# Stick-breaking attention of a two-block fp32 kernel: TensorE's order alternates from step to step, and the weighing moves two steps behind the transposes

## The chip, the cores and the metric

The kernel runs on one core of one Trainium2 chip. The metric is the device time of one execution in microseconds (us). One execution runs two transformer-like blocks over 2048 tokens of width 1024, all in float32; the change touches one stage of the first block, the stick-breaking attention.

## The reference, cut to the stage that changes

```python
SEQ, N_HEADS, HEAD_DIM, Q_BLOCK = 2048, 8, 64, 128

def _stick_breaking_attention(q, k, v):
    ...
    for blk in range(n_blocks):
        q0 = blk * Q_BLOCK
        kl = q0 + Q_BLOCK
        qb = qf[:, :, q0:kl]
        z = jnp.einsum("bhqd,bhkd->bhqk", qb, kf[:, :, :kl]) * scale
        q_pos = q0 + jnp.arange(Q_BLOCK)
        mask = jnp.arange(kl)[None, :] < q_pos[:, None]
        log_one_minus = jnp.where(mask, jax.nn.log_sigmoid(-z), 0.0)
        rev = lax.cumsum(log_one_minus, axis=3, reverse=True)
        weights = jnp.exp(jnp.where(mask, z + rev, -jnp.inf))
        outs.append(jnp.einsum("bhqk,bhkd->bhqd", weights, vf[:, :, :kl]))
    ...

def first_block(...):
    ...  # a gated short convolution, then k, v, q and g by projections
    o = _stick_breaking_attention(q, k, v)
    x = x + (o * jax.nn.silu(g)) @ w_out_b[j]
    return _rmsnorm(x, norm_f)
```

The kernel uses that the running product of sigmoid(-z) from the right, P, gives the weights as differences P(k+1) - P(k). It multiplies P with differences of neighbouring values instead, so the weights themselves are never formed.

## The kernel before

The kernel runs its stages one after another: the mixer (Strassen products), its output product, projections, then **the stick-breaking stage** (`phase_stick`), the stage's output product, the second block's projection, its selection and attention, and the last output product.

In the stick-breaking stage the 8 heads are taken as 4 *head pairs*. For each head pair the 16 blocks of 128 queries follow each other, and the keys of a block are cut into chunks of at most 512, the one with the diagonal first. One (head pair, query block, chunk) is a **unit**: 40 per head pair, 160 in all. Counted from a head pair's start, units 0, 1, 2, 3 are blocks of one unit each with 128, 256, 384 and 512 keys; blocks of two units follow (unit 4 has 128 keys and unit 5 has 512; 6 and 7 have 256 and 512; and so on), then blocks of three from unit 12 and of four from unit 24. A block's first unit *opens* it and its last one *closes* it; only the first of a block can be shorter than 512. The last unit of the head pair before is called unit -1 here.

Each unit passes five engines' hands, for its two heads (`s` = 0, 1):

1. **scores** on TensorE (L1650): three products of split fp32 parts for each of two heads, into one of four PSUM buffers `z`;
2. **soften** on ScalarE (L1525): sigmoid from `z` into `soft`; for the unit that opens a block GpSimd then masks the diagonal (L1504);
3. **multiply** on VectorE (L1598): a scan over the unit for each head, `soft` into `prod`, with the carry of the unit before it in the block;
4. **transposes** on TensorE (L1668) of `prod` into `turn`, and **leave** on ScalarE (L1534) from there into `prob`;
5. **weighing** on TensorE (L1689): `prob` with the values' differences into the block's output `o_ps`. There are two such PSUM buffers, one for even and one for odd blocks. When a block is closed, VectorE copies it out with an addition (`leave` in its section, L1608, "the copy-out" below). The weighing of a unit that opens block b waits for the copy-out of block b-2 (`o_left`).

Every engine's section is a loop over steps `t`, written out in order; an engine executes its list in that order and waits on semaphores. Before, step t of TensorE is: scores(t+2), transposes(t), at some steps transposes of values, weighing(t-1). ScalarE's step is soften(t+2), leave(t); VectorE's is multiply(t+1), and copy-out(t-2) where unit t-2 closes a block. So scores run two steps ahead of the transposes.

Four times per head pair, at steps 4 and 12 of it and 8 and 5 steps before its start, a quarter of the keys, queries and values is prepared (`chores_at`): ScalarE makes `k_hi`, `q_hi` at the end of the step (L1516, L1518), VectorE makes `k_lo`, `q_lo`, `v_step` (L1574, L1576, L1580), and a step later TensorE transposes the values (`transpose_v`, L1676, "values' transposes" below) through the same two `turn` buffers. `turn_free` makes each use of a `turn` buffer wait until ScalarE has emptied the one two uses before.

Of the kernel before, what the change touches and what calls it, by code (L numbers as in the profile page):

```python
# [1360 lines left out]
def phase_stick(nc, sem, kvqg_t, o_t, ident, loaded, space, w_out_b, x1, mod_row, norm_w, head_norms):  # L1361
# [11 lines left out]
    U = len(units)  # L1373
# [8 lines left out]
    def closes(u):  # L1382
        return units[u][2] == 0
# [27 lines left out]
    with ExitStack() as ctx:  # L1411
# [95 lines left out]
        @block.scalar  # L1507
        def _(act):
            nc.scalar.preload_act_table(ACT.Sigmoid)

            def split(n, pair, piece):
                j, cols = pair % 2, piece_cols(piece)
                if pair >= 2:
                    act.wait_ge(z_ready, 2 * EACH * (pair - 1))
                act.wait_ge(k_in[piece], 16 * (pair + 1))
                nc.scalar.activation(k_hi[:, j, cols], k_raw[:, cols], ACT.Copy).then_inc(kh_done, 1)  # L1516
                act.wait_ge(q_in[piece], 16 * (pair + 1))
                nc.scalar.activation(q_hi[:, j, cols], q_raw[:, cols], ACT.Copy).then_inc(qh_done, 1)  # L1518

            def soften(u, s):  # L1520
                n = units[u][3]
                act.wait_ge(z_ready, 2 * u + s + 1)
                if u >= DEEP:
                    act.wait_ge(multiplied, 2 * (u - DEEP) + s + 1)
                nc.scalar.activation(soft[:, u % DEEP, s, 0:n], z[u % 2 * 2 + s][:, 0:n], ACT.Sigmoid, scale=-SCALE).then_inc(softened, 1)  # L1525

            def leave(u, s):
                n = units[u][3]
                act.wait_ge(turned, 2 * u + s + 1)
                if u == 0:  # L1530
                    act.wait_ge(loaded.upper_out, 16 * TILES)
                if u >= DEEP:
                    act.wait_ge(weighed, u - DEEP + 1)
                nc.scalar.activation(prob[:, u % DEEP, s, 0:n], turn[turn_of["unit", u, s] % 2][:, 0:n], ACT.Copy).then_inc(p_ready, 1)  # L1534

            def leave_v(n, pair, piece):
                act.wait_ge(v_turned, n + 1)
                if pair >= 2:
                    act.wait_ge(weighed, EACH * (pair - 1))
                nc.scalar.activation(v_nat[:, pair % 2, piece * 4:piece * 4 + 4].rearrange("p a b -> p (a b)"),  # L1540
                                     turn[turn_of["v", n] % 2][:], ACT.Copy).then_inc(v_left, 1)

            def split_weights(k):
                act.wait_ge(space.w_in[k], 16)
                nc.scalar.activation(space.w_hi[:, k], space.w_raw[:, k], ACT.Copy).then_inc(space.w_hi_done, 1)

            for t in range(-2, U + 2):
                if t in weights_at:
                    split_weights(weights_at.index(t))
                if t in outputs_at:  # L1550
                    space.high(nc, act, outputs_at.index(t))
                if t == -2:
                    for c in chores_at(t):
                        split(*c)
                if 0 <= t + 2 < U:
                    for s in range(2):
                        soften(t + 2, s)
                if 0 <= t < U:
                    for s in range(2):
                        leave(t, s)  # L1560
                for c in chores_at(t - 1):
                    leave_v(*c)
                if t > -2:
                    for c in chores_at(t):
                        split(*c)

        @block.vector
        def _(dve):
# [31 lines left out]
            def leave(u):  # L1600
                pair, qb, _, _ = units[u]
                j, last = pair % 2, P * (qb + 1)
                dve.wait_ge(weighed, u + 1)
                if u == 0:
                    dve.wait_ge(loaded.lower_out, 16 * TILES)
                if pair >= 2:
                    dve.wait_ge(o_out[qb * P // PIECE], 16 * (pair - 1))
                nc.vector.tensor_scalar(o_sb[:, j, qb * P:last], o_ps[block_of[u] % 2][:, 0:P], v_raw[:, j, last:last + 1], None,  # L1608
                                        ALU.add).then_inc(o_left, 1)
# [2 lines left out]
                dve.wait_ge(space.w_hi_done, k + 1)  # L1612
                nc.vector.tensor_tensor(space.w_lo[:, k], space.w_raw[:, k], space.w_hi[:, k].bitcast(F32), ALU.subtract).then_inc(space.w_lo_done, 1)

            for t in range(-2, U + 2):
                if t == weights_at[0]:
                    dve.wait_ge(space.cols_in, 48)
                    nc.vector.scalar_tensor_tensor(space.cols[:, 0], space.cols[:, 0], 1.0, space.cols[:, 1], ALU.add, ALU.mult).then_inc(space.scale_made, 1)
                if t - 1 in weights_at:
                    split_weights(weights_at.index(t - 1))  # L1620
                if t + 1 in outputs_at:
                    space.gate(nc, dve, outputs_at.index(t + 1))
                if t - 1 in outputs_at:
                    space.low(nc, dve, outputs_at.index(t - 1))
                if t == -2:
                    for c in chores_at(t):
                        split(*c)
                if 0 <= t + 1 < U:
                    for s in range(2):
                        multiply(t + 1, s)  # L1630
                if 0 <= t - 2 < U and closes(t - 2):
                    leave(t - 2)
                if t > -2:
                    for c in chores_at(t):
                        split(*c)

        @block.tensor
        def _(pe):
# [40 lines left out]
            def weigh(u):  # L1679
                pair, qb, at, n = units[u]  # L1680
                o = o_ps[block_of[u] % 2]
                pe.wait_ge(p_ready, 2 * u + 2)
                pe.wait_ge(v_left, pair * PIECES + qb * P // PIECE + 1)
                if opens(u) and block_of[u] >= 2:
                    pe.wait_ge(o_left, block_of[u] - 1)
                for c in range(0, n, P):
                    for s in range(2):
                        rows_s = slice(s * HD, s * HD + HD)
                        ins = nc.tensor.matmul(o[rows_s, 0:P], v_nat[:, pair % 2, (at + c) // P, rows_s], prob[:, u % DEEP, s, c:c + P],  # L1689
                                               start=opens(u) and c == 0, stop=closes(u) and c + P == n)  # L1690
                ins.then_inc(weighed, 1)

            for t in range(-2, U + 2):
                if 0 <= t + 2 < U:
                    scores(t + 2)
                if 0 <= t < U:
                    for s in range(2):
                        transpose(t, s)
                for c in chores_at(t - 1):
                    transpose_v(*c)  # L1700
                if 0 <= t - 1 < U:
                    weigh(t - 1)


def phase_out_b(nc, sem, space, x1, o_t, kvqg_t, norm_f, ident, xf, xt_hi, xt_lo, xt_raw, next_w, next_ps):
# [1742 lines left out]
```

## Time and profile before

| what | us |
|---|---|
| median of 3 runs | 3191.09 |
| lowest and highest run | 3189.61, 3191.92 |
| span of the profiled execution | 3189.0 |
| TensorE busy in the span (matmuls) | 2990.2 |
| VectorE busy | 2253.7 |
| ScalarE busy | 1624.1 |
| stick-breaking stage, first scores to the last weighing | 1198.1 to 1641.5 |

The profiled execution's own span is 2.1 us under the median of the runs. The stage takes 443.4 us of it, 14%. TensorE's rows come as matmuls (PE) and weight loads (PEld). A matmul's end is modelled, so for the pace of TensorE the starts are read, and best those of the weight loads: each matmul has one, and the distance from the first load of one group to the first load of the next is the time that the group takes. In the profile the weighing shows two hardware matmuls for each one of the program.

### The profile page before, as it was taken

The numbers are of one execution on the slowest core, as the hardware profiler recorded it, in microseconds if no ns is written. First come the engines' busy times: TensorE is split into PE (matmuls) and PEld (weight loads), VectorE is DVE, ScalarE is ACT, GpSimd is POOL, SyncE is SP. The second block draws the span as 40 slices with busy tenths as digits, with TensorE's granted clock in tenths as the row PEclk, the third lists the DMA queues.
The fourth block names the chain that finished last, engine by engine and source line by source line (L and its number), as shares of the span: only waits on it lengthen the run. The fifth ranks groups of instructions, "written<-read, shape, count | busy, mean of one in ns | idle before, by whom it ended". The sixth has DMA issues, their size and how long they took to land. (4 is left out here: it accounts for less than half of the span.)

```text
span 3189.0 us, 48176 instructions
## 1 busy us (share of the span) xinstructions
PE 2990.2 (94%) x17460; PEld 2369.3 (74%) x17460; DVE 2253.7 (71%) x3296; ACT 1624.1 (51%) x2947; POOL 231.3 (7%) x519
## 2 busy tenths in 40 slices
PE   6999999999998999999999999999977889998899
PEld 5888788888777866677777777887756666776687
DVE  8888877753677758888878554524378989988543
ACT  5344422232545436777769423211288887887500
POOL 0000000000000001110100000000021321213100
PEclk8999999999999999999999999999989999999899
DMA  4434422244657432111136334232641111011665
GB/s 119 121 109 122 145 67 75 84 141 144 170 171 254 154 131 77 32 37 41 45 92 199 112 96 132 86 132 74 172 98 34 31 28 24 23 36 39 170 183 158
DMA packets 377860, 331.47 MB, mean 104 GB/s; under 512 B 100988, under 2 KB 331900, under 8 KB 371472
## 3 DMA queue, kind: packets, MB, share of 16 engines
q1 hardware_dynamic: 371784, 293.40, 32.4%
q0 software_dynamic: 5120, 34.67, 2.8%
q8 instruction: 142, 2.33, 0.3%
q14 instruction: 94, 0.77, 0.1%
q10 hardware_dynamic: 720, 0.31, 0.1%
HBM read 211.26 MB, written 107.10 MB: 100 GB/s over the span
## 5 line engine op out<-in xcount | busy, mean ns | idle before, releaser
L629 PE MATMUL p_oa_acc<-s_h_a_hi,s_mx_w_hi 128*128 128x512 f32 x768 | 301.8, 393 | 15.2 <-DVE s_h_a_lo L418 9.4
L323 ACT ACTIVATE s_mx_w_hi<-s_mx_raw 128x512 fp32r<-128x512 f32 x224 | 139.1, 629 | 320.6 <-PE p_oa_acc L629 256.8
L629 PE MATMUL p_oa_acc<-s_h_a_lo,s_mx_w_hi 128*128 128x512 f32 x768 | 300.4, 391 | 0.0
L629 PE MATMUL p_oa_acc<-s_h_a_hi,s_mx_w_lo 128*128 128x512 f32 x768 | 300.2, 391 | 0.0
L1598 DVE TENSOR_TENSOR_SCAN s_st_prod<-s_st_soft,s_st_prod 128x512 f32<-128x512 f32 x192 | 234.4, 1267 | 15.9 <-ACT s_st_soft L1525 15.9
L3174 PE MATMUL p_sa_turn<-s_ident,s_sa_arg 128*128 128x128 f32 x1088 | 166.3, 289 | 48.5 <-ACT s_sa_prob L2783 30.9
L1525 ACT ACTIVATE s_st_soft<-p_st_z 128x512 f32<-128x512 f32 (+3 forms) x320 | 153.7, 534 | 112.0 <-PE p_st_z L1650 112.0
L2345 PE MATMUL p_pr_ps<-s_h_hi,s_pr_w_hi 128*128 128x512 f32 (+1 forms) x712 | 195.4, 395 | 1.8 <-PEq L1712 1.2
L2766 ACT ACTIVATE s_sa_arg<-s_sa_arg,s_sa_low_top 128x128 f32<-128x128 f32 (+15 forms) x128 | 155.7, 1218 | 79.6 <-DVE s_sa_low_top L2918 79.6
L460 DVE TENSOR_TENSOR s_mx_w_lo<-s_mx_raw,s_mx_w_hi 128x512 fp32r<-128x512 f32 x224 | 153.5, 685 | 57.8 <-ACT s_mx_w_hi L323 56.3
L2345 PE MATMUL p_pr_ps<-s_h_lo,s_pr_w_hi 128*128 128x512 f32 (+1 forms) x712 | 191.5, 389 | 0.0
L2345 PE MATMUL p_pr_ps<-s_h_hi,s_pr_w_lo 128*128 128x512 f32 (+1 forms) x712 | 191.5, 389 | 0.0
L3174 PEld LDWEIGHTS p_sa_turn<-s_ident,s_sa_arg 128*128 128x128 f32 x1088 | 120.9, 145 | 86.4 <-issue 53.3
L2227 DVE TENSOR_TENSOR s_pr_w_lo<-s_pr_raw,s_pr_w_hi 128x1024 fp32r<-128x1024 f32 (+1 forms) x22 | 26.5, 1204 | 223.5 <-ACT s_pr_w_hi L2168 223.5
L629 PEld LDWEIGHTS p_oa_acc<-s_h_a_hi,s_mx_w_hi 128*128 128x128 f32 x768 | 145.0, 189 | 47.9 <-issue 17.9
L2775 ACT ACTIVATE s_sa_relu<-p_sa_pr 128x512 f32<-128x512 f32 (+3 forms) x304 | 155.5, 567 | 28.0 <-DVE s_sa_score L2899 13.8
L629 PEld LDWEIGHTS p_oa_acc<-s_h_a_hi,s_mx_w_lo 128*128 128x128 f32 x768 | 145.1, 189 | 30.4
L3188 PE MATMUL p_sa_o_sum<-s_sa_prob,s_sa_v_nat 128*64 128x128 f32 x2176 | 160.7, 288 | 7.4 <-ACT s_sa_o L2789 7.4
L629 PEld LDWEIGHTS p_oa_acc<-s_h_a_lo,s_mx_w_hi 128*128 128x128 f32 x768 | 145.2, 189 | 29.6
L2899 DVE SCALAR_TENSOR_TENSOR s_sa_score<-s_sa_relu,s_sa_w_idx,s_sa_score 128x1024 f32<-128x1024 f32 (+7 forms) x154 | 153.8, 1021 | 18.9 <-ACT s_sa_relu L2775 17.9
L3188 PEld LDWEIGHTS p_sa_o_sum<-s_sa_prob,s_sa_v_nat 128*64 128x64 f32 x2176 | 121.2, 141 | 58.9 <-issue 46.3
L2783 ACT ACTIVATE s_sa_prob<-p_sa_turn 128x512 f32<-128x512 f32 (+3 forms) x320 | 154.3, 541 | 11.2 <-PE p_sa_turn L3174 10.7
(379 smaller groups left out, 7408.7 us busy)
## 6 DMA issues: line engine op xcount, KB each, us to landing
s_mx_raw<-in_w_in_a SPq DMA_DIRECT2D x128, 256.0 KB, 3.8
s_pb_ada<-in_w_ada SPq DMA_DIRECT2D x16, 768.0 KB, 4.3
s_pr_raw<-in_w_in SPq DMA_DIRECT2D x21, 512.0 KB, 3.9
s_pr_work<-s_pr_stage SPq DMA_DIRECT2D x38, 256.0 KB, 4.2
d_rot_hi<-s_pr_rot POOLq DMA_DIRECT2D x9, 1024.0 KB, 4.3
d_rot_lo<-s_pr_stage POOLq DMA_DIRECT2D x9, 1024.0 KB, 6.2
d_y_t<-s_mx_y SPq DMA_DIRECT2D x16, 512.0 KB, 5.5
s_oa_y_raw<-d_y_t SPq DMA_DIRECT2D x16, 512.0 KB, 4.8
```

The source lines that it names most:

```text
L323: nc.scalar.activation(w_hi[:, m], raw[g % 2][:, m], ACT.Copy).then_inc(hi_done, 1)
L460: nc.vector.tensor_tensor(w_lo[:, m], raw[g % 2][:, m], w_hi[:, m].bitcast(F32), ALU.subtract).then_inc(lo_done, 1)
L629: ins = nc.tensor.matmul(bank, w[:, m, k, :], a[:, m, k, :], start=(k == 0 and n == 0), stop=(k == KH - 1 and n == 2))
L1525: nc.scalar.activation(soft[:, u % DEEP, s, 0:n], z[u % 2 * 2 + s][:, 0:n], ACT.Sigmoid, scale=-SCALE).then_inc(softened, 1)
L1598: nc.vector.tensor_tensor_scan(prod[:, b, s, 0:n][:, ::-1], back, back, carry, ALU.mult, ALU.bypass).then_inc(multiplied, 1)
L2345: ins = nc.tensor.matmul(ps[b % 2][0:cols, t * 512:(t + 1) * 512], w[b % 2][:, k, 0:cols], a[:, k, t * 512:(t + 1) * 512], start=(k == 0 a ...
L2766: nc.scalar.activation(row, row, ACT.Exp, scale=-1.0, bias=low_top[:, s % DEEP, side, len(parts(qb)) - 1:len(parts(qb))], accum_out=total[ ...
L2775: nc.scalar.activation(relu[:, a % R_DEEP, half:half + n], pr[p % BANKS][:, 0:n], ACT.Relu).then_inc(relu_done, 1)
L2783: nc.scalar.activation(prob[:, u % P_DEEP, side, 0:w], turn[turn_of["prob", u, side] % 2][:, 0:w], ACT.Copy).then_inc(p_ready, 1)
L2899: ins = nc.vector.scalar_tensor_tensor(s, relu[:, a % R_DEEP, 0:n], w, s, ALU.mult, ALU.add)
L3174: ins = nc.tensor.transpose(turn[i % 2][:, c:c + P], arg[:, s % DEEP, side, at + c:at + c + P], ident[:])
L3188: ins = nc.tensor.matmul(o_ps[side * HD:side * HD + HD, pair * P:pair * P + P], v_nat[:, (at + c) // P, kv * HD:kv * HD + HD], prob[:, u % ...
```

## The change

TensorE's steps alternate. At even t the order is scores(t+2), transposes(t), weighing(t-2); at odd t it is weighing(t-2), transposes(t), scores(t+2). The weighing is one step later than it was. ScalarE's order follows: at odd t soften(t+2) stands behind leave(t). VectorE's copy-out moves from step t = u+2 to t = u+3 for a unit u, so one more pair of scans stands ahead of it. No instruction is added or removed, and sizes, buffers and semaphore targets stay.

```diff
@@ scalar
-                if 0 <= t + 2 < U:
+                if 0 <= t + 2 < U and t % 2 == 0:
                     for s in range(2):
                         soften(t + 2, s)
                 if 0 <= t < U:
@@
                 for c in chores_at(t - 1):
                     leave_v(*c)
+                if 0 <= t + 2 < U and t % 2:
+                    for s in range(2):
+                        soften(t + 2, s)
@@ vector
-            for t in range(-2, U + 2):
+            for t in range(-2, U + 3):
@@
-                if 0 <= t - 2 < U and closes(t - 2):
-                    leave(t - 2)
+                if 0 <= t - 3 < U and closes(t - 3):
+                    leave(t - 3)
@@ tensor
             for t in range(-2, U + 2):
-                if 0 <= t + 2 < U:
+                if 0 <= t - 2 < U and t % 2:
+                    weigh(t - 2)
+                if 0 <= t + 2 < U and t % 2 == 0:
                     scores(t + 2)
                 if 0 <= t < U:
                     for s in range(2):
                         transpose(t, s)
                 for c in chores_at(t - 1):
                     transpose_v(*c)
-                if 0 <= t - 1 < U:
-                    weigh(t - 1)
+                if 0 <= t + 2 < U and t % 2:
+                    scores(t + 2)
+                if 0 <= t - 2 < U and t % 2 == 0:
+                    weigh(t - 2)
```

The first place is TensorE at the start of a head pair (line numbers of the changed kernel are 3 higher). `p_st_z` are scores, `p_st_turn` transposes, `p_st_o` the weighing; a unit of 128 keys has 2 transposes and 2 weighing products, one of 512 has 8 of each. Before, from the transposes of unit 1 to the weighing of unit 2:

```order
L1668 MATMUL p_st_turn<-s_ident,s_st_prod 128x128 x4
L1689 MATMUL p_st_o<-s_st_prob,s_st_v_nat 64x128 x2
L1650 MATMUL p_st_z<-s_st_k_hi,s_st_q_hi 128x128 x2
L1650 MATMUL p_st_z<-s_st_k_lo,s_st_q_hi 128x128 x2
L1650 MATMUL p_st_z<-s_st_k_hi,s_st_q_lo 128x128 x2
L1668 MATMUL p_st_turn<-s_ident,s_st_prod 128x128 x6
L1689 MATMUL p_st_o<-s_st_prob,s_st_v_nat 64x128 x4
L1650 MATMUL p_st_z<-s_st_k_hi,s_st_q_hi 128x512 x2
L1650 MATMUL p_st_z<-s_st_k_lo,s_st_q_hi 128x512 x2
L1650 MATMUL p_st_z<-s_st_k_hi,s_st_q_lo 128x512 x2
L1668 MATMUL p_st_turn<-s_ident,s_st_prod 128x128 x8
L1689 MATMUL p_st_o<-s_st_prob,s_st_v_nat 64x128 x6
```

The same engine and place after the change, from the transposes of unit 1 to those of unit 3:

```order
L1671 MATMUL p_st_turn<-s_ident,s_st_prod 128x128 x4
L1653 MATMUL p_st_z<-s_st_k_hi,s_st_q_hi 128x512 x2
L1653 MATMUL p_st_z<-s_st_k_lo,s_st_q_hi 128x512 x2
L1653 MATMUL p_st_z<-s_st_k_hi,s_st_q_lo 128x512 x2
L1653 MATMUL p_st_z<-s_st_k_hi,s_st_q_hi 128x128 x2
L1653 MATMUL p_st_z<-s_st_k_lo,s_st_q_hi 128x128 x2
L1653 MATMUL p_st_z<-s_st_k_hi,s_st_q_lo 128x128 x2
L1671 MATMUL p_st_turn<-s_ident,s_st_prod 128x128 x6
L1692 MATMUL p_st_o<-s_st_prob,s_st_v_nat 64x128 x6
L1671 MATMUL p_st_turn<-s_ident,s_st_prod 128x128 x8
```

The scores of units 3 and 4 now stand together, and so do the weighings of units 0 and 1 (2 and 4 products in one row of 6); the weighing of unit 1 stands ahead of the transposes of unit 3.

The second place is VectorE there: `s_st_prod` are the scans (two in a row for one unit, 128, 256, 384, 512, 128 and 512 keys), `s_st_o` the copy-outs of units -1, 0 and 1. Before:

```order
L1598 SCALAR_TENSOR_TENSOR s_st_prod<-s_st_soft 128x256 x2
L1598 SCALAR_TENSOR_TENSOR s_st_prod<-s_st_soft 128x384 x2
L1608 TENSOR_SCALAR s_st_o<-p_st_o,s_st_v_raw 128x128
L1598 SCALAR_TENSOR_TENSOR s_st_prod<-s_st_soft 128x512 x2
L1608 TENSOR_SCALAR s_st_o<-p_st_o,s_st_v_raw 128x128
L1598 SCALAR_TENSOR_TENSOR s_st_prod<-s_st_soft 128x128 x2
L1608 TENSOR_SCALAR s_st_o<-p_st_o,s_st_v_raw 128x128
L1598 SCALAR_TENSOR_TENSOR s_st_prod<-s_st_soft,s_st_prod 128x512 x2
```

After:

```order
L1601 SCALAR_TENSOR_TENSOR s_st_prod<-s_st_soft 128x256 x2
L1601 SCALAR_TENSOR_TENSOR s_st_prod<-s_st_soft 128x384 x2
L1601 SCALAR_TENSOR_TENSOR s_st_prod<-s_st_soft 128x512 x2
L1611 TENSOR_SCALAR s_st_o<-p_st_o,s_st_v_raw 128x128
L1601 SCALAR_TENSOR_TENSOR s_st_prod<-s_st_soft 128x128 x2
L1611 TENSOR_SCALAR s_st_o<-p_st_o,s_st_v_raw 128x128
L1601 SCALAR_TENSOR_TENSOR s_st_prod<-s_st_soft,s_st_prod 128x512 x2
L1611 TENSOR_SCALAR s_st_o<-p_st_o,s_st_v_raw 128x128
```

The copy-out of unit -1 now stands behind the scans of unit 3, and that of unit 1 behind those of unit 5.

## Rows read from the trace of the kernel before

**Rows 1.** The page's first part: busy us (share) xinstructions of each engine.

```profile
PE 2990.2 (94%) x17460; PEld 2369.3 (74%) x17460; DVE 2253.7 (71%) x3296; ACT 1624.1 (51%) x2947; POOL 231.3 (7%) x519
```

**Rows 2.** Busy time by stretch: the stage, then its second and third head pair.

```profile
core 0: us, PE busy (x) PEld busy (x) DVE busy (x) ACT busy (x) POOL busy (x), PEclk, DMA share, GB/s
1198.10:1641.50 443.40, 428.77 (x4288) 315.72 (x4288) 379.47 (x438) 319.26 (x692) 42.31 (x64) 0.99 0.15 42
1311.68:1422.70 111.02, 106.60 (x1074) 78.36 (x1072) 97.98 (x115) 82.48 (x176) 12.88 (x16) 1.00 0.16 40
1422.70:1533.70 111.00, 107.57 (x1084) 79.26 (x1083) 93.91 (x110) 79.80 (x175) 10.43 (x17) 1.00 0.14 39
```

**Rows 3.** Waits in the stage: us in total, times, longest us.

```profile
ACT s_st_soft L1525 <- PE p_st_z L1650: 112.0, 138, 1.9
...
PEld p_st_turn L1676 <- ACT s_st_prob L1534: 16.9, 15, 1.7
...
PE p_st_turn L1676 <- DVE s_st_v_step L1580: 6.6, 5, 1.4
```

**Rows 4.** Timeline, one full step: start us, us, engine, line, operation, xcount.

```profile
1589.54 4.79 DVE L1598 TENSOR_TENSOR_SCAN s_st_prod<-s_st_soft,s_st_prod 128x512 f32<-128x512 f32 x4
...
1590.23 0.19 PEld L1650 LDWEIGHTS p_st_z<-s_st_k_hi,s_st_q_hi 64*128 64x128 f32 x2 [0.17 <-issue]
...
1590.57 0.39 PE L1650 MATMUL p_st_z<-s_st_k_lo,s_st_q_hi 64*128 64x512 f32 x2
1590.57 0.19 PEld L1650 LDWEIGHTS p_st_z<-s_st_k_hi,s_st_q_lo 64*128 64x128 f32 x2
1590.80 0.39 PE L1650 MATMUL p_st_z<-s_st_k_hi,s_st_q_lo 64*128 64x512 f32 x2
1591.13 0.86 PEld L1668 LDWEIGHTS p_st_turn<-s_ident,s_st_prod 128*128 128x128 f32 x8 [0.37 <-issue]
...
1591.23 1.09 ACT L1525 ACTIVATE s_st_soft<-p_st_z 128x512 f32<-128x512 f32 x2 [0.88 <-PE p_st_z L1650]
1592.15 0.85 PEld L1689 LDWEIGHTS p_st_o<-s_st_prob,s_st_v_nat 128*64 128x64 f32 x16 [0.17 <-issue]
...
1593.17 0.19 PEld L1650 LDWEIGHTS p_st_z<-s_st_k_hi,s_st_q_hi 64*128 64x128 f32 x2 [0.17 <-issue]
```

**Rows 5.** Timeline, the stage's end, where no scores are left.

```profile
1636.72 0.86 PEld L1668 LDWEIGHTS p_st_turn<-s_ident,s_st_prod 128*128 128x128 f32 x8 [0.17 <-issue]
...
1637.74 0.85 PEld L1689 LDWEIGHTS p_st_o<-s_st_prob,s_st_v_nat 128*64 128x64 f32 x16 [0.17 <-issue]
...
1639.79 1.73 PEld L1689 LDWEIGHTS p_st_o<-s_st_prob,s_st_v_nat 128*64 128x64 f32 x32 [0.17 <-issue]
```

**Rows 6.** Timeline, scores behind transposes: the stage's start, and the selection stage.

```profile
1199.72 0.72 PEld L1676 LDWEIGHTS p_st_turn<-s_ident,s_st_v_step 128*128 128x128 f32 x4 [0.22 <-issue]
...
1200.77 0.29 PEld L1650 LDWEIGHTS p_st_z<-s_st_k_hi,s_st_q_hi 64*128 64x128 f32 x2 [0.33 <-issue]
...
2700.36 1.09 PE L3174 MATMUL p_sa_turn<-s_ident,s_sa_arg 128*128 128x128 f32 x8
2701.21 0.48 PE L3152 MATMUL p_sa_pr<-s_sa_ki_qi_q 128*128 128x512 f32 x1
```

**Rows 7.** Timeline, the second head pair's start.

```profile
1311.68 1.09 PE L1668 MATMUL p_st_turn<-s_ident,s_st_prod 128*128 128x128 f32 x8
...
1316.84 1.09 ACT L1525 ACTIVATE s_st_soft<-p_st_z 128x512 f32<-128x512 f32 x2 [1.07 <-PE p_st_z L1650]
...
1318.57 2.50 DVE L1598 TENSOR_TENSOR_SCAN s_st_prod<-s_st_soft 128x512 f32<-128x512 f32 x2 [0.45 <-issue]
1320.99 0.32 DVE L1608 TENSOR_SCALAR s_st_o<-p_st_o,s_st_v_raw 128x128 f32<-128x128 f32 x1
...
1325.44 1.09 PE L1668 MATMUL p_st_turn<-s_ident,s_st_prod 128*128 128x128 f32 x8
1327.17 0.66 PE L1676 MATMUL p_st_turn<-s_ident,s_st_v_step 128*128 128x128 f32 x4 [0.64 <-ACT s_st_prob L1534]
```

## The prediction, made before the changed kernel was run

> **What bounds the kernel now.** I read the page's engine part first: TensorE is busy 94% of the span, VectorE 71% [rows 1]. Then the stretches of the stage: in its 443.4 us TensorE's matmuls fill 428.8 and VectorE 379.5 [rows 2]. TensorE is the bound, but VectorE has only 64 us to spare in 160 steps. Then the waits: the only waits of TensorE that matter are for the values' transposes, some 16.9 us behind ScalarE's emptying of `turn` (the weight loads' wait, the matmuls' own is shorter) and 6.6 us behind `v_step` [rows 3]. That agrees with the stretches: 443.4 - 428.8 = 14.6 us of idle, about 1 us for each of the 16 values' transposes. ScalarE waits 112 us for scores, so it follows TensorE [rows 3].
>
> Last, one full step. The loads start at 1590.23 (scores), 1591.13 (transposes), 1592.15 (weighing), 1593.17 (next scores): a step of 2.94 us [rows 4]. Within a group a score product takes 0.23 us (1590.57 to 1590.80), a transpose 0.86 / 8 = 0.107, a weighing 0.85 / 16 = 0.053. So the groups need 3 x 0.23 = 0.70, 0.86 and 0.85, together 2.41, and 0.53 to 0.55 us are **seams** between unlike groups: scores to transposes 0.10, transposes to weighing 0.17 (1592.15 - 1591.13 - 0.86), weighing to scores 0.17, and a late second product in the scores (0.34 from the group's start instead of 0.23), 0.11.
>
> Also seen there: VectorE runs four scans from 1589.54 to 1594.33, while the scores at 1590.23 are two units ahead of the transposes at 1591.13. VectorE has made the product that is transposed about a step before it is wanted, a **lead** of 2 to 3 us.
>
> **The change part by part.** *Seams.* Two steps have six seams before. After: scores-transposes-weighing, weighing-transposes-scores; two like groups stand together twice. Weighing behind weighing costs nothing: 32 loads take 1.73 us, twice 0.85 and 0.03 [rows 5]. Scores behind scores have no row at the full clock; the products inside a group follow at 0.23 with their loads hidden behind the product before (load at 1590.57 while the product of 1590.57 streams) [rows 4], so I take 0, and as the other end the 0.11 of a fresh group. Weighing to transposes is 0.17 [rows 5]. Transposes to scores: in the selection stage 0.85 from 8 transposes to the scores, seam 0 [rows 6]; at this stage's start four transposes take 1.05 us at half pace, where 4 x 0.213 (twice 0.107) = 0.85 would do, seam 0.20 [rows 6]. The latter are the same instructions, so I take 0.17, with 0 as the other end. New pair of steps: 0.10 + 0.17 + 0.17 + (0.17 + 0.11) = 0.72 against 2 x 0.55 = 1.10. **Gain 0.38 us per two steps, 80 pairs: -30.4 us**; ends -22 (scores behind scores 0.11) and -44 (transposes to scores 0). The order of the stage's last few groups hardly changes, so there is no added drain.
>
> The trace shows 0.17 wherever transposes (128 x 128 tile) and weighing (128 x 64) or weighing and scores (64 x 128) meet, and none between two 128 x 128 forms [rows 5, 6]. The Trainium skill, TensorEngine Tiling (Array Packing), Key Properties, says that a change of tiling mode drains TensorE. By that rule transposes to scores costs a seam here too; it speaks for the 0.17 and not for the 0.
>
> *Lead.* Before, the scores of unit u stand two whole steps ahead of its transposes. Now, for odd u, they stand at the end of a step: scores(u), scores(u+1), transposes(u-1), two weighings, transposes(u). From a score group's start to the soften is 1.00 us (1590.23 to 1591.23), the two softens take 1.09, so a scan can start some 0.6 behind the first one's start, and two scans take 2.4 to 2.5 (4.79 for four) [rows 4, 7]. So transposes(u) can have both heads 1.0 + 0.6 + 2.5 = 4.1 us after scores(u) started, and TensorE reaches them after 0.81 + 0.80 + 0.86 + 0.17 + 1.70 + 0.17 = 4.5, and the second head after 4.9. In full steps it just holds, with 0.4 to 0.9 us to spare where it was 2 to 3. VectorE needs 4.9 to 5.2 us of the 5.5 that two steps now take, so it holds on average too. Where a pair of scans meets a mask, a copy-out or odd sizes, 0.3 to 0.4 us of wait appear; following the order unit by unit I find about five such places per head pair, 1.4 us: **+5.6 us**.
>
> *The copy-out behind the scans.* This is the large one. Take a head pair's start, 0 = transposes of unit -1 (in the trace at 1311.68). Shorter units are scaled: transposes and weighing by their keys, the three score products 0.32, 0.34 and 0.54 for 128, 256 and 384 keys (0.23 x keys / 512, but no less than the 0.107 of a load). TensorE: scores of 1 and 2 at 1.03 and 1.48, transposes of 0 at 2.12, weighing of -2 and -1 from 2.50 to 4.20, transposes of 1 at 4.37, scores of 3 at 4.97 and of 4 at 5.78, transposes of 2 at 6.20, weighing of 0 at 7.01. Weighing of 1 could start at 7.22; it opens a block, so it needs the copy-out of unit -1. That stands behind the scans of unit 3: soften 5.97 to 7.06, mask, scans from 7.70 (0.64 behind the softens' end, as 1317.93 to 1318.57) to 10.1, copy 0.33 [rows 7]. Weighing of 1 starts at 10.5: **wait 3.3 us**. Then transposes of 3 at 11.1, scores of 5 at 12.1; weighing of 3 could start at 14.4 but needs the copy-out of unit 1, behind the scans of unit 5, which run from 13.7 to 16.1: start 16.5, **wait 2.1 us**. Transposes of 5 come at 17.5, where before they came 1325.44 - 1311.68 = 13.8 after the start [rows 7]. Queued behind the waiting weighing on TensorE are the transposes and scores of that step, and with them ScalarE. Units 2 and 4 open blocks too, but at even steps their weighing comes late enough, and later blocks have two or more units. 5.3 us for three head pairs; in the first one there is no unit -1 and only the second wait comes, 2.1: **+18 us**.
>
> *Values' transposes.* At odd steps they stand ahead of the scores, at even ones as before. Three of four per head pair stay at about their wait of 1 to 1.5 us, as `v_step` still ends it: k_hi and q_hi come behind the same leave. The fourth (prepared 5 steps before the head pair's end) now finds ScalarE with soften(u+2) ahead of the splitting, by my walk 2.2 us instead of 1.2. Three of those and small change: **+4 us**. The soften moved behind leave at odd steps costs nothing by itself: ScalarE is busy 319 of 443 us [rows 2]. No DMA moves; SP's waits are on copy-outs and splittings a few us later, with quarters of a head pair to spare.
>
> Sum: -30.4 + 5.6 + 18 + 4 = **-2.8 us**, rounded to -2. The profiled execution's span becomes 3187, and with the 2.1 us between span and median, **3189 us**. Unknowns: seams -14 to +8, and the waits, where my walk may be wrong by a third of 28, 9 us either way.
>
> **Rivals.**
>
> *Free seam from transposes to scores.* For it, the selection stage's row with no gap [rows 6]; against it, that the scores there use all 128 rows, and the half-pace row. 80 x 0.17 = 13.6 us more gain, of which a third falls into VectorE's pace: 3189 - 9 = 3180.
>
> *The copy-out waits are smaller than walked.* If the mask and scans of units 3 and 5 come sooner, or what TensorE loses there is given back at the values' transposes that follow (the 0.87 between the transposes' last load, 1325.44 + 0.86, and 1327.17 [rows 7] would vanish, which I have only partly counted), 12 to 16 us of the 28 go: 3175.
>
> *VectorE becomes the bound.* With the lead gone, each lump on VectorE (three splitting operations, 2 us, 16 times; 64 copy-outs; 64 masks) reaches TensorE instead of being swallowed. For it, 4.9 to 5.2 us of work in 5.5 and a margin of 0.4 us; against it, that TensorE already waits once per lump and VectorE catches up there. It decides from the point where the loop scores(u) to transposes(u) of full odd units needs over 4.9 us instead of 4.1; each 0.1 above costs 8 us over 80 pairs, and one more us at each of the 16 splittings costs 16. 3189 + 16 = 3205, slower than before.
>
> *Scores behind scores pay like a fresh group*: 80 x 0.11 = 9 us: 3198. What the trace shows is a load that starts while the product on the same rows of the array streams [rows 4]. The Trainium skill, TensorE: Matmul & The Clock Gate, Part 3, says that a weight load overlaps a running matmul only when the row groups differ. By that rule this rival would hold; within a group the trace disagrees with it, so it gets little.
>
> *The change doesn't do what it says*: the listing shows the groups regrouped as meant, so none.
>
> **How the numbers follow.** Forecast 0.44, on its own 3183 to 3196. Free seam 0.17, small waits 0.12, VectorE the bound 0.20, dear scores 0.07. A measurement of this kernel can tell about 0.2%, 6.4 us, from no change: 3184.7 to 3197.5. Faster: 0.17 + 0.12 and a little of the forecast's edge, 0.30. Slower: 0.20 + 0.07, 0.27. Within: 0.43. The range goes from 3176, leaving most of the small waits out, to 3204, leaving out half of VectorE the bound.
>
> **What would show it.** In the changed trace: step pairs of full units 5.5 us long instead of 5.88, with loads 0.17 apart between transposes and scores and the six score products at one pace of 0.23; weighings of 32 loads in a row. A wait of the weighing for the copy-out (L1611) of 2 to 3.5 us, seven times. Scans waited for by transposes for a few us in all. The stage at about 441 us. Wrong would be: no such wait for the copy-out, or waits of transposes for scans above 15 us in all, or step pairs under 5.35 us. If the stage ends below 430 us, the waits were overrated; above 455, the lead was.

## The result and the profile after

The changed kernel takes 3209.87 us (median of 4 runs, 3208.93 to 3211.5) against 3190.35 us for the kernel before (4 runs, 3188.99 to 3191.92): 1.0062 times as long, 95% interval 1.0050 to 1.0075. It is slower by 20 us, where 3189 was forecast and 3204 was the top of the range.

All of it lies in the stage. From its first scores to the table load on ScalarE that opens the next stage it takes 1200.38 to 1666.29, 465.9 us; before it took 444.8 by the same marks. The page's first part and the stage's stretch of the changed kernel (columns as in [rows 2]):

```profile
PE 2977.7 (93%) x17460; PEld 2383.1 (74%) x17460; DVE 2254.9 (70%) x3296; ACT 1624.4 (51%) x2947; POOL 232.7 (7%) x519
```

```profile
1200.38:1666.29 465.91, 419.50 (x4288) 332.54 (x4288) 381.36 (x439) 321.93 (x692) 45.12 (x64) 0.96 0.14 39
```

The numbers of instructions are those of [rows 1, 2]. TensorE is busy 9 us less than in [rows 2]. A matmul's modelled end runs into the seam behind it (eight transposes last 1.09 us as matmuls and 0.86 as loads), so fewer seams show as less busy time. But it stands idle for 46 us instead of 15. And the granted clock of the stage is 0.96 where it was 0.99. That last number is what the prediction had no term for.

**The seams.** Timeline of the changed kernel, late in the stage (columns as in [rows 4]):

```profile
1652.28 0.19 PEld L1653 LDWEIGHTS p_st_z<-s_st_k_hi,s_st_q_hi 64*128 64x128 f32 x2 [0.17 <-issue]
...
1652.62 0.19 PEld L1653 LDWEIGHTS p_st_z<-s_st_k_hi,s_st_q_lo 64*128 64x128 f32 x2
1652.85 0.19 PEld L1653 LDWEIGHTS p_st_z<-s_st_k_hi,s_st_q_hi 64*128 64x128 f32 x2
1653.08 0.19 PEld L1653 LDWEIGHTS p_st_z<-s_st_k_lo,s_st_q_hi 64*128 64x128 f32 x2
...
1653.86 0.91 PEld L1671 LDWEIGHTS p_st_turn<-s_ident,s_st_prod 128*128 128x128 f32 x8 [0.36 <-issue]
1654.94 1.73 PEld L1692 LDWEIGHTS p_st_o<-s_st_prob,s_st_v_nat 128*64 128x64 f32 x32 [0.17 <-issue]
...
1656.84 0.86 PEld L1671 LDWEIGHTS p_st_turn<-s_ident,s_st_prod 128*128 128x128 f32 x8 [0.17 <-ACT s_st_prob L1534]
...
1657.86 0.19 PEld L1653 LDWEIGHTS p_st_z<-s_st_k_hi,s_st_q_hi 64*128 64x128 f32 x2 [0.17 <-issue]
```

The loads of the second unit's scores start at 1652.85, 0.23 us behind the load before them and 0.23 us ahead of the next one, with no fresh start: scores behind scores cost nothing. 32 weighing loads run in one piece, as in [rows 5]. From transposes to scores it is 1657.86 - 1656.84 - 0.86 = 0.16 us. So the two seams that no row of before showed for these forms at full clock came out at the values taken, 0 and 0.17. The whole pair of full steps, 1652.28 to 1657.86, takes 5.58 us, of which 0.06 us lie in its first transposes (1.08 us to the next group, 1.02 elsewhere); before it took 2 x 2.94 = 5.88 us [rows 4]. The gain is 0.30 to 0.35 us a pair, 24 to 28 us for 80 pairs, a little under the 0.38 taken: that sum started from seams of 0.55 us a step, while 2.94 - 2.41 is 0.53, and had 1.87 us for the double weighing and its seam, which takes 1.90. The rule cited from the Trainium skill's TensorEngine Tiling (Array Packing), Key Properties, holds for this seam, and the free seam of the selection stage was no guide.

**The waits.** Waits of the changed kernel's stage (waiter, what it waited for, us in total, times, longest), to be read against [rows 3]:

```profile
PEld p_st_turn L1679 <- ACT s_st_prob L1534: 20.4, 15, 2.2
PE p_st_o L1692 <- DVE s_st_o L1611: 17.9, 7, 3.1
...
PE p_st_turn L1679 <- DVE s_st_v_step L1583: 10.5, 8, 1.8
PE p_st_turn L1671 <- DVE s_st_prod L1601: 8.8, 26, 0.8
PE p_st_turn L1679 <- ACT s_st_prob L1534: 6.5, 5, 2.0
```

The weighing waits for the copy-out seven times, 17.9 us, where the prediction walked to seven waits and 18. The values' transposes wait 17.1 us (10.5 + 6.5, rounded) instead of 13.5 (6.9 behind the emptying of `turn` and 6.6 behind `v_step`), by the matmuls' own waits. The transposes of units wait 8.8 us for scans, 26 times, where it was 1.0, and another 1.3 us for `prob` and `v_nat`.

**The clock.** Here is the second head pair's start, the place of [rows 7] (timeline of the changed kernel):

```profile
1316.18 1.09 PE L1671 MATMUL p_st_turn<-s_ident,s_st_prod 128*128 128x128 f32 x8
...
1323.43 0.44 PE L1692 MATMUL p_st_o<-s_st_prob,s_st_v_nat 128*64 128x128 f32 x4
...
1324.17 2.46 DVE L1601 TENSOR_TENSOR_SCAN s_st_prod<-s_st_soft 128x512 f32<-128x512 f32 x2 [1.51 <-ACT s_st_soft L1525]
1326.55 0.32 DVE L1611 TENSOR_SCALAR s_st_o<-p_st_o,s_st_v_raw 128x128 f32<-128x128 f32 x1
...
1327.01 0.79 PE L1692 MATMUL p_st_o<-s_st_prob,s_st_v_nat 128*64 128x128 f32 x8 [3.15 <-DVE s_st_o L1611]
...
1327.73 1.57 PEld L1671 LDWEIGHTS p_st_turn<-s_ident,s_st_prod 128*128 128x128 f32 x8 [0.31 <-issue]
...
1329.63 0.29 PEld L1653 LDWEIGHTS p_st_z<-s_st_k_hi,s_st_q_hi 64*128 64x128 f32 x2 [0.33 <-issue]
1329.63 0.79 PE L1653 MATMUL p_st_z<-s_st_k_hi,s_st_q_hi 64*128 64x512 f32 x2
```

The copy-out at 1326.55 stands behind the scans of unit 3, and the weighing of unit 1 waits for it for 3.15 us, as walked. What comes then was not foreseen: eight transposes and the way to the next group take 1.90 us (1327.73 to 1329.63) instead of 1.03, so they run at half pace. The stretches say why (columns as in [rows 2]; the eighth number is the granted clock):

```profile
1320.00:1324.00 4.00, 3.75 (x38) 2.58 (x34) 2.66 (x4) 2.33 (x7) 0.33 (x1) 1.00 0.00 0
1324.00:1328.00 4.00, 0.99 (x9) 0.71 (x10) 3.59 (x6) 0.64 (x2) 0.44 (x2) 0.93 0.07 27
1328.00:1332.00 4.00, 4.00 (x26) 3.13 (x27) 0.21 (x1) 2.04 (x4) 0.00 (x0) 0.65 0.79 178
```

The granted clock was at its full level, 2.4 GHz, until TensorE stood idle; it fell to the 1.2 GHz level at the wait's end and stayed there until about 1331. Taking the stage from its first scores in stretches of 4 us and adding (1 - clock) x 2 x their length gives the time at the lower level ("half clock" below): 9.8 us before, all of it at the stage's start, and **35.0 us after**: 7 to 8 at the stage's start, and eight drops of some 3.4 us each, one at the second head pair's start (1324), two at each of the next two (1444 and 1560, behind both waits), and three at values' transposes (1304, 1424, 1540). Two of the seven copy-out waits, of 2.1 us in the first and second head pair, had no drop behind them. The Trainium skill's TensorE: Matmul & The Clock Gate, Part 1, says that the clock is the engine's answer to its own recent idleness; the trace agrees, here with a drop behind an idle of 3 us in a stage that is otherwise dense.

### The profile page after: what moved, and what is told of

Read it like the earlier page. It is cut to its first block and busy times, and to the rows that moved or that the text cites. A ratio compares the mean times of both kernels' runs of the same rounds, so it can differ in the third digit from the quotient of the medians.

```text
span 3209.7 us, 48176 instructions
## 1 busy us (share of the span) xinstructions
PE 2977.7 (93%) x17460; PEld 2383.1 (74%) x17460; DVE 2254.9 (70%) x3296; ACT 1624.4 (51%) x2947; POOL 232.7 (7%) x519
## 5 line engine op out<-in xcount | busy, mean ns | idle before, releaser
L1534 ACT ACTIVATE s_st_prob<-p_st_turn 128x512 f32<-128x512 f32 (+3 forms) x320 | 158.4, 551 | 104.4 <-PE p_st_turn L1671 103.5
L1671 PE MATMUL p_st_turn<-s_ident,s_st_prod 128*128 128x128 f32 x1088 | 163.6, 287 | 10.2 <-DVE s_st_prod L1601 8.8
L2782 ACT ACTIVATE s_sa_relu<-p_sa_pr 128x512 f32<-128x512 f32 (+3 forms) x304 | 155.5, 565 | 28.9 <-PE p_sa_pr L3160 14.7
L2906 DVE SCALAR_TENSOR_TENSOR s_sa_score<-s_sa_relu,s_sa_w_idx,s_sa_score 128x1024 f32<-128x1024 f32 (+7 forms) x154 | 153.7, 1021 | 18.8 <-ACT s_sa_relu L2782 17.8
```

The costliest lines, as they stand in the source:

```text
L1671: ins = nc.tensor.transpose(turn[i % 2][:, c:c + P], prod[:, u % DEEP, s, c:c + P], ident[:])
L2782: nc.scalar.activation(relu[:, a % R_DEEP, half:half + n], pr[p % BANKS][:, 0:n], ACT.Relu).then_inc(relu_done, 1)
L2906: ins = nc.vector.scalar_tensor_tensor(s, relu[:, a % R_DEEP, 0:n], w, s, ALU.mult, ALU.add)
```

## The experiments

All "stage" times below go from the first scores to the table load, as above (before 444.8, after 465.9), each from one profiled execution; the kernel of experiment 8, profiled twice, gave 437.0 and 435.8 us, with 15.8 and 11.0 us at half clock. The rest of the execution, whose code no edit touches, takes 2741 to 2747 us in the profiles with the true scans, so whole times and stages differ by a few us in what they say. The ratios are against the kernel before run beside each experiment, whose medians were 3191.33 us for experiments 1 to 4, 3189.11 for 5 to 8 and 3188.22 for 9 to 11. Counts of waits are the matmuls' own.

**1. The copy-outs of odd units early again** (in the changed kernel, VectorE's section):

```diff
-                if 0 <= t - 3 < U and closes(t - 3):
-                    leave(t - 3)
+                for u in (t - 3, t - 2):
+                    if 0 <= u < U and closes(u) and t - u == (2 if u % 2 else 3):
+                        leave(u)
```

> The changed kernel, but the copy-outs of odd units stand one step earlier again (unit u at step u+2; even units stay at u+3). Theory 'waits and clock': the seven waits of the weighing for the copy-out (17.9 us in the changed trace) go, and with them the stretches at half clock that follow them (about 2 us at each head pair's start, 6 to 7 us in all): 3184 to 3187. Theory 'waits alone': 3192, with the half-clock stretches still there or worth nothing. Theory 'lost lead': the time comes back as waits of the transposes for the scans, and it stays above 3200.

Measured: 3193.76 us, 1.0005 of before (0.9995 to 1.0016), stage 450.9, so 15 us less than after. The time at half clock falls to 27.9 us. Its waits:

```profile
PE p_st_turn L1672 <- DVE s_st_prod L1601: 13.1, 29, 1.4
PE p_st_turn L1680 <- DVE s_st_v_step L1583: 12.7, 11, 1.8
PE p_st_turn L1680 <- ACT s_st_prob L1534: 6.8, 4, 2.0
```

No wait for the copy-out is left, but the transposes now wait 13.1 us for scans instead of 8.8, with one of 1.4 us: at a head pair's start the transposes of unit 3 need the very scans behind which the copy-out stood. The total misses the 3184 to 3187 of 'waits and clock' and comes nearest to the 3192 of 'waits alone', but its half clock moved, so it decides between neither: 18 us of waits and 7 us at half clock went, 6.5 us of waits came back at scans and `v_step`. 'Lost lead' had named that return and put it far too high.

**2. One splitting moved by a step**, so that its values' transposes fall on an odd step:

```diff
-        return pair * EACH + (-8, -5, 4, 12)[piece]
+        return pair * EACH + (-8, -4, 4, 12)[piece]
```

> The changed kernel, but the splitting that stood 5 steps before a head pair's end stands 4 steps before it, so that its values' transposes fall on an odd step, behind which ScalarE empties first. Theory 'waits and clock': three waits fall from 2.0 to about 1 us and the half pace behind them (a weighing of 32 in 3.0 us instead of 1.9, 1.1 to 1.5 us each) goes: 6 to 8 us less, 3202 to 3204. Theory 'waits alone': 3 us less, 3207. Theory 'lost lead': no change, 3210, since VectorE's work is the same.

Measured: 3203.35 us, 1.0034 of before (1.0023 to 1.0045), stage 457.5, 8.4 less than after. Half clock 28.9 us, and none of it at the values' transposes any more. The total is what 'waits and clock' said. In the changed kernel the place looked so (timeline, third head pair coming):

```profile
1423.44 1.09 PE L1671 MATMUL p_st_turn<-s_ident,s_st_prod 128*128 128x128 f32 x8
1426.52 1.09 PE L1679 MATMUL p_st_turn<-s_ident,s_st_v_step 128*128 128x128 f32 x4 [1.99 <-ACT s_st_prob L1534]
1427.53 3.06 PE L1692 MATMUL p_st_o<-s_st_prob,s_st_v_nat 128*64 128x128 f32 x32
1430.52 1.09 PE L1671 MATMUL p_st_turn<-s_ident,s_st_prod 128*128 128x128 f32 x8
```

A wait of 2.0 us, and 32 weighing products that take 1427.53 to 1430.52, 2.99 us, instead of 1.90 with their seam. Here the wait was in the prediction (2.2 us, "small change" behind it) and what it set off was not.

**3. Both edits.**

> Both edits together. Theory 'waits and clock': the gains add, 3177 to 3180, under the kernel before (3190). Theory 'waits alone': 3189. Theory 'lost lead': above 3195.

Measured: 3188.3 us, 0.9993 of before (0.9982 to 1.0004), stage 445.4, 20.5 less than after where the two edits alone gave 15.0 and 8.4; half clock 17.8 us. So the gains nearly add; it is experiment 1 that had brought less than 'waits and clock' expected. The total came out where 'waits alone' had put it, but not for its reason: the half clock fell as well, while waits for `v_step` rose to 17.5 us and those for scans to 13.7, against 10.5 and 8.8 in the changed kernel (the values' waits for `prob`, 6.5 us, are gone). Both count: what TensorE loses at the clock it loses on top, and what it no longer loses at the copy-out it partly waits for at VectorE.

**4. Work in the waits.** What releases the waiting weighing stays as it was; only TensorE does not stand idle:

```diff
+            def weigh_again(u, times):
+                ...
                 if 0 <= t - 2 < U and t % 2:
+                    if t >= 3 and again(t - 3):
+                        weigh_again(t - 3, 12 if units[t - 3][3] == P else 2)
                     weigh(t - 2)
```

`weigh_again(u, times)` issues the products of `weigh(u)` so many times over, into the same block's output. `again(u)` is true for units 0 and 2 of a head pair where the unit behind them waits for a copy-out. The signal that these two units are weighed moves behind the repeats.

> The changed kernel with TensorE kept at work in the copy-out waits: ahead of the two waiting weighings of each head pair it weighs the unit before once more (12 times for the one of 128 keys, 2.6 us; twice for the one of 384, 1.3 us), which writes the same numbers. The waits for the copy-out themselves stay, shorter by what fills them. Theory 'waits and clock': the granted clock stays up behind the waits, the transposes of unit 3 take 0.9 us instead of 1.7 and the scores behind them 0.8 instead of 1.2: 5 to 8 us less, 3202 to 3205. Theories 'waits alone' and 'lost lead': no gain, 3210, since the work that releases the wait is VectorE's and ScalarE's.

Measured: 3203.22 us, 1.0034 of before (1.0024 to 1.0045), stage 454.6: **11.3 us less than after, with 240 matmuls more** (4528 in the stage instead of 4288). The same stretches as above, of this kernel:

```profile
1320.00:1324.00 4.00, 4.00 (x50) 3.46 (x52) 2.49 (x3) 2.87 (x8) 0.77 (x2) 1.00 0.02 4
1324.00:1328.00 4.00, 3.47 (x46) 2.88 (x44) 2.64 (x6) 0.82 (x2) 0.00 (x0) 1.00 0.30 99
1328.00:1332.00 4.00, 3.32 (x50) 2.68 (x46) 2.86 (x4) 3.27 (x9) 0.41 (x1) 1.00 0.76 150
```

And its timeline, where the transposes of unit 3 start at 1326.49 and the scores behind them at 1327.51, 1.02 us on, not 1.90:

```profile
1315.07 1.09 PE L1671 MATMUL p_st_turn<-s_ident,s_st_prod 128*128 128x128 f32 x8
...
1322.58 2.79 PE L1707 MATMUL p_st_o<-s_st_prob,s_st_v_nat 128*64 128x128 f32 x48
1325.90 0.66 PE L1695 MATMUL p_st_o<-s_st_prob,s_st_v_nat 128*64 128x128 f32 x8 [0.53 <-DVE s_st_o L1611]
1326.49 1.09 PE L1671 MATMUL p_st_turn<-s_ident,s_st_prod 128*128 128x128 f32 x8
1327.51 0.50 PE L1653 MATMUL p_st_z<-s_st_k_hi,s_st_q_hi 64*128 64x512 f32 x2
```

The time at half clock in the stage falls from 35.0 to 17.1 us. This is the run that separates the clock from the waits. The first waiting weighing is released as late as ever (1325.90 behind transposes of unit -1 at 1315.07, 10.8 us, as 1327.01 behind 1316.18, 10.8 us, in the changed kernel), and still what follows comes sooner: from the transposes of unit -1 to those of unit 6 the changed kernel takes 23.0, 24.0 and 24.0 us at its three later head pairs, this one 21.5, 21.2 and 21.2. That is 7.2 us of the 11.3 in the filled places alone. The rest can't be put to the filling: the stretches at the three values' transposes came out at the full level too, which no edit touched (one at 1356 came instead, behind an idle stretch of 1.61 us, and the stage's start had 6 us more). Over the whole execution the gain is 6.7 us by the medians.

The traces also show what half clock costs. Against the changed kernel, count each us of wait less as one and each us at half clock less as a half:

| experiment | waits, us less | half clock, us less | counted | stage measured, us less |
|---|---|---|---|---|
| 1 | 11.1 | 7.1 | 14.7 | 15.0 |
| 2 | 4.3 | 6.1 | 7.4 | 8.4 |
| 3 | 12.5 | 17.2 | 21.1 | 20.5 |
| 4 (filled waits left out) | 1.8 | 17.9 | 10.8 | 11.3 |

Within about 1 us the two together give the stage; the waits alone give it in no row.

**5. The late copy-out alone**, in the kernel before, with TensorE's and ScalarE's old orders:

```diff
-                if 0 <= t - 2 < U and closes(t - 2):
-                    leave(t - 2)
+                if 0 <= t - 3 < U and closes(t - 3):
+                    leave(t - 3)
```

> The kernel before with one part of the change alone: VectorE's copy-out one step later (u+3), TensorE's and ScalarE's orders as before. At a head pair's start the weighing of unit 1 could start 1319.06 and the copy-out of unit -1 would end behind the scans of unit 3 at 1321.3; the weighing of unit 3 could start at 1323.5 plus that wait, its copy-out behind the scans of unit 5. Theory 'copy-out behind scans': waits of 2.2 and about 1 us, 10 to 13 us in all with some half pace behind them: 3201 to 3204, and the stage 10 to 13 us longer than 445. Rival 'it only hurts in the turned order': waits under 3 us in all, 3191 to 3193.

Measured: 3201.36 us, 1.0042 of before (1.0029 to 1.0054), stage 458.1, 13.3 more than before.

```profile
PE p_st_o L1689 <- DVE s_st_o L1608: 7.8, 5, 2.3
```

Only 7.8 us of it are waits for the copy-out; the half clock is 20.2 us where it was 9.8, and waits for `prob` (1.5 us) follow. So one line of the change costs 12 us by itself (3201.36 against 3189.11), and the rival that it would only hurt in the turned order is out.

**6 and 7. VectorE taken out of the play.** Each scan is replaced by an elementwise product of the same size, in the kernel before and in the kernel of experiment 3. The running product is left out, so the numbers are others; on them the selection stage executes 62 reductions of some 1.7 us on VectorE that the kernel before does not (L3003), and the whole takes some 3400 us. Only the stage is compared; the expected totals, which left this out, say nothing.

```diff
-                nc.vector.tensor_tensor_scan(prod[:, b, s, 0:n][:, ::-1], back, back, carry, ALU.mult, ALU.bypass).then_inc(multiplied, 1)
+                nc.vector.tensor_tensor(prod[:, b, s, 0:n], soft[:, b, s, 0:n], soft[:, b, s, 0:n], ALU.mult).then_inc(multiplied, 1)
```

> The kernel before with each scan replaced by a product of the same size (soft times itself, about 0.6 to 0.7 us for 512 instead of 1.2): the running product is left out, so the numbers are other ones and only the time counts. VectorE then has 170 us less work in the stage. TensorE was the bound: the stage 440 to 444 us where it was 445, 3187 to 3191, by every theory.

> The turned order with both edits of c_both (copy-outs of odd units early, splitting 4 steps ahead) and the scans replaced by a product as in g_short_before (running product left out). Theory 'the seams are 0.38 us per two steps and the lost lead swallows them': 28 to 32 us under g_short_before, 3157 to 3162, and no waits of transposes for VectorE's products. Rival 'the seams give less than that, whatever VectorE does': under 20 us, 3170 or more.

Measured: 3399.45 and 3381.75 us; stages 442.7 and 424.3. In the old order the stage hardly moves (-2.1 us for 146 us less of VectorE), in the turned one it loses 21 us against experiment 3. The difference of the two is 18.3 us, not the 28 to 32 of the expectation. The turned one's waits tell the rest:

```profile
PE p_st_turn L1680 <- DVE s_st_v_step L1583: 17.2, 15, 1.7
...
PE p_st_turn L1672 <- DVE s_st_prod L1601: 2.5, 3, 0.8
PE p_st_turn L1672 <- ACT s_st_prob L1534: 1.1, 4, 0.4
```

Together 20.8 us (with 13.5 for the values in the old order), so 7 us more of waits, and 12.3 instead of 9.9 us at half clock. 18.3 + 7.3 + half of 2.4 is 27, inside the 24 to 28 of the seams. The expectation had counted no such waits: those for the values end with the splitting, which stays, and a few for VectorE's products were left too.

**8. `v_step` ahead of `k_lo` and `q_lo`** in VectorE's splitting, on top of experiment 3 (`step()` is the three removed statements, waits included; `n` is 0 for the very first piece):

```diff
+                if n:
+                    step()
                 dve.wait_ge(kh_done, n + 1)
                 nc.vector.tensor_tensor(k_lo[:, j, cols], ...
                 dve.wait_ge(qh_done, n + 1)
                 nc.vector.tensor_tensor(q_lo[:, j, cols], ...
-                dve.wait_ge(v_in[piece], 16 * (pair + 1))
-                ...
+                if not n:
+                    step()
```

> c_both with VectorE making v_step ahead of k_lo and q_lo at each splitting (the first one excepted), so that the values' transposes don't wait for the splits of keys and queries, which in turn wait for ScalarE. Theory 'lumps on VectorE reach TensorE': the waits for v_step (17.5 us) fall by 10 to 15 us, some of it comes back as waits for scans: 3178 to 3184. Rival 'the waits only move': 3186 to 3190, since VectorE's work is the same and its scans come as late as before.

Measured: **3180.82 us, 0.9973 of before (0.9963 to 0.9984)**, stage 437.0. Its waits:

```profile
PE p_st_turn L1678 <- DVE s_st_prod L1607: 15.3, 32, 1.4
PE p_st_turn L1686 <- ACT s_st_prob L1534: 4.2, 12, 1.1
PE p_st_turn L1678 <- ACT s_st_prob L1534: 3.1, 7, 0.6
```

The wait for `v_step` is gone, 17.5 us; some 8 us of it are gained, and the rest comes back as waits for `prob` (7.3 us where it was 1.1) and for scans (15.3 where it was 13.7). The clock still falls once, at 1320, behind idle stretches of only 1.36 and 0.49 us.

**9 to 11. The control, a finer split, and experiment 8 again.**

> Control: the kernel before with nothing but v_step ahead of k_lo and q_lo at each splitting. Theory 'lumps on VectorE reach TensorE at the values' transposes in either order': the waits for v_step (6.6 us) go, those for the emptying of turn stay: 3184 to 3187. If it gives as much as c_vfirst (3181), the turned order brings nothing even when mended.

> c_vfirst with q_lo made one step later than v_step and k_lo, so that VectorE's lump is split over two steps (from the second head pair's pieces on). Theory 'with little lead a lump costs what exceeds the margin': waits for scans 3 to 5 us fewer than the 15.3 us of c_vfirst, 3176 to 3179. Rival 'only VectorE's sum counts': 3180 to 3182.

> c_vfirst once more beside the two others, for its interval against the control: 3179 to 3182, the stage about 437 us.

Experiment 9 makes the same edit in the kernel before, experiment 10 moves `q_lo` to the next step, on top of experiment 8:

```diff
+                for n, pair, piece in chores_at(t - 1):
+                    if n >= PIECES:
+                        lows(n, piece, pair % 2, piece_cols(piece), False, True)
```

Measured: the control 3186.77 us, 0.9993 of before (0.9984 to 1.0002), stage 443.8; the finer split 3180.1 us, 0.9973 (0.9964 to 0.9982), stage 435.4; experiment 8 again 3180.42 us, 0.998 (0.997 to 0.999), stage 435.8. So `v_step` first is worth nothing that can be told in the old order, and the mended turned order is 6 us under its control, its stage 8 us. The finer split brings no more: waits for scans fall to 13.2 us, 2 and not 3 to 5, but those for `v_step` come back with 3.9. Its total is where 'only VectorE's sum counts' had put it. That VectorE sets the pace is not shown by it: VectorE is busy 379 us of the stage's 435, TensorE's matmuls 410.

## Why the prediction was wrong

Step by step, against what the change did to the stage (forecast -2.8 us, measured 465.9 - 444.8 = +21.1):

- **Seams, -30.4.** Right in kind, a little large. A pair of full steps fell from 5.88 us to 5.53 to 5.58, so -24 to -28; experiments 6 and 7 give 27 once waits and clock are set apart.
- **The copy-out behind the scans, +18.** Right in mechanism, number (seven), places and size (17.9), down to the 3.3 and 2.1 us walked (3.15 and 2.16 us measured in the second head pair).
- **Values' transposes, +4.** Right as a wait: 17.1 against 13.5.
- **Lead, +5.6.** Too small. The waits for scans are 8.8 against 1.0, +7.8, and for `prob` and `v_nat` +1.3 more. The walk left out the four weight-splitting operations on VectorE in the second head pair (three of 1.2 us and one of 1.4). By the starts of its transposes that head pair took 119.5 us, 8.4 more than before, the third one 116.1, 6.2 more than its 109.9.
- **The clock, no term.** This is the step that failed. With the measured sizes, -28 + 17.9 + 3.6 + 9.1 = +2.6 (+6.6 with seams of -24), and the stage grew by 21.1. 25 us more of it ran at the lower level; each such us costs half of one, by the table under experiment 4, so the drops are worth 12.6 us. Another 2 to 6 us stay open. In experiments 6 and 7, where VectorE's scans are short, seams, waits and clock account for all of the difference; between the control and experiment 11, with the full scans, 6 to 10 us are open too. So the open part goes with VectorE's full work; what it is was not measured.

The walk priced each wait at its length and let TensorE come back at full pace. It had the other pace before its eyes, in the row of the stage's start that it read as half pace ([rows 6]), and drew no term from it. Behind the wait at 1327 the eight transposes took 0.88 us more than at full clock and the scores behind them 0.53 more (1.77 instead of 1.24); a whole drop of 3.4 us costs 1.7. Where the clock stayed up, the walk was good: it put the transposes of unit 5 17.5 us behind those of unit -1, and they came after 18.1 us in experiment 4 and 19.7 in the changed kernel. Charged with 1.4 to 1.7 us at each of its ten waits of 2 us and more (seven copy-outs, three values' transposes), the forecast would have been 3203 to 3206, still 4 to 7 us short of the 3209.87 measured, with drops behind eight of the ten.

Of the prediction's signs, its waits for the copy-out came, the waits for scans stayed under 15 us and the step pairs over 5.35. The last sign, a stage above 455 us, came true and was to mean that the lead was overrated. It was, by the 3.5 us between +5.6 and +9.1; the clock is the larger part.

Of the rivals, 'VectorE becomes the bound' had the right sign and came nearest (3205), but not by its mechanism: the full pair shown holds its pace, and the margin was eaten at lumps. 'Small waits' is out, since the 3.15 us wait was there in full, and so are the free seam and the dear scores. The range missed because its width came from seams and the lengths of waits alone. That its upper end was missed by only 6 us is no credit to it: half of VectorE as the bound, which it was drawn for, is not what happened.

## What to carry to other kernels

In a stage that TensorE bounds, a new wait of 2 to 3 us can cost more than its length, since TensorE may come back at half clock, here for some 3.4 us worth 1.7; where a wait can't be removed, harmless work in it can pay (with 240 extra matmuls this stage was 11 us shorter, 7 of them where the work was put). Turning an order round to save seams takes the lead of the producers away on every second step: before that, look at what each engine has queued behind its long operations, and here above all at short ones, such as the copy-out of a buffer, that stood in the right place. One line of the change, the late copy-out, cost 12 us by itself; with it put back for odd units, one splitting moved and `v_step` made first, the turned order is 0.2 to 0.3% faster than the kernel before.

## What the runs showed of the hardware that was not expected

- The granted clock fell behind a single idle stretch of TensorE of 3.15 us (3.36 by the weight loads) up to 1327.0, and of 1.99 us (2.2 by the loads) up to 1426.5, in a stage where it was busy 90% of the time; the stretches there add up to 3.4 us at the lower level each, by the same sum as above. No length of wait tells it apart. It stayed up behind copy-out waits of 2.16 us in the changed kernel and behind three waits of 2 us at values' transposes in experiment 4, and fell behind 1.61 us in experiment 4, behind 1.36 and 0.49 us close together in experiments 1 and 8, and behind 0.45 and 1.16 us close together in experiment 1. Behind idle stretches of up to 1.3 us from 1212 on in the kernel before it never fell.
- At the lower level transposes are paced at 0.2 us instead of 0.107, full score products at 0.42 to 0.43 instead of 0.23.
- A seam costs 0.16 to 0.17 us where the array's tile changes (128 x 128, 128 x 64 and 64 x 128 here, in any order but scores to transposes, 0.10), and nothing where two units of one kind follow each other, though there are semaphore waits between them.
